# Tap matrices of a depthwise convolution: laid out on the host and loaded by GpSimd's queue, in place of a VectorE product

## What is computed

```
def _causal_depthwise_conv(x, w):
    k = w.shape[0]
    return lax.conv_general_dilated(
        x, w[:, None, :], window_strides=(1,), padding=[(k - 1, 0)],
        dimension_numbers=("NWC", "WIO", "NWC"), feature_group_count=x.shape[-1])
...
def conformer_conv(x, w_in, w_dw, b_dw, ln_g, ln_b, w_out):
    a, gate = jnp.split(x @ w_in, 2, axis=-1)
    u = a * jax.nn.sigmoid(gate)
    u = _causal_depthwise_conv(u, w_dw) + b_dw
    u = jax.nn.silu(_layer_norm_2(u, ln_g, ln_b))
    return u @ w_out
```

## Time and profile before

| | |
|---|---|
| runs, median (lowest to highest) | 1764.91 us (1762.72 to 1766.04) |
| the profiled execution's own time | 1764.59 us |
| its span in the trace | 1762.6 us |
| granted TensorE clock, mean | 0.975 of full speed |
| TensorE (PE) busy | 1657.1 us, 94% |
| VectorE (DVE) busy | 1373.8 us, 78% |
| ScalarE (ACT) busy | 1031.0 us, 58% |
| GpSimd (POOL) busy | 48.3 us, 3% |

### The profile page before, as it was taken

The page is one execution under the profiler, slowest core; times in us unless marked ns, Lnnn a source line. Parts: engine busy times, 40 slices in busy tenths (PEclk is TensorE's granted clock), DMA queues, the critical chain, the costliest instruction groups (busy, mean ns, idle before and its releaser), DMA issues.

```text
span 1762.6 us, 22524 instructions
## 1 busy us (share of the span) xinstructions
PE 1657.1 (94%) x9022; PEld 1378.5 (78%) x9022; DVE 1373.8 (78%) x1252; ACT 1031.0 (58%) x901; POOL 48.3 (3%) x44
## 2 busy tenths in 40 slices
PE   2999999988989999998899999999999999999976
PEld 2988678868869998896788777887778877788754
DVE  7786666675875555668788989989899898988986
ACT  2344344463324333434577887778887788877862
POOL 0000002000000000000100000000000000000010
PEclk8999999999999999999899999999999999999998
DMA  9688245704745646453799999999999999999992
GB/s 365 224 338 332 96 155 190 288 1 159 205 177 209 251 157 237 180 215 144 267 404 370 408 414 418 406 388 416 415 415 409 399 408 405 417 408 378 411 413 98
DMA packets 119663, 528.30 MB, mean 300 GB/s; under 512 B 10288, under 2 KB 16704, under 8 KB 76288
## 3 DMA queue, kind: packets, MB, share of 16 engines
q1 hardware_dynamic: 112704, 512.44, 74.9%
q10 hardware_dynamic: 5520, 9.62, 1.5%
q0 software_dynamic: 1328, 4.73, 0.7%
HBM read 519.84 MB, written 14.25 MB: 303 GB/s over the span
## 4 chain that ended last, share of the span: by engine, by line
PE 59%; DVE 11%; DMA 5%; ACT 3%; issue 1%; POOL 0%; SPq 0%; DVEq 0%; POOLq 0%; ACTq 0%
PE psum L932 15%; PE psum L934 15%; PE psum L933 15%; DVE units L2029 7%; DMA ring<-in_experts 5%; PE psum L1348 3%; PE psum L1349 2%; ACT units L1838 2%; PE psum L1411 1%; PE psum L1259 1%; PE psum L1463 1%; PE psum L1370 1%; PE psum L1400 1%; DVE R L2429 0%; PE psum L1212 0%
## 5 line engine op out<-in xcount | busy, mean ns | idle before, releaser
L2029 DVE TENSOR_TENSOR units<-ring,units 128x2048 fp32r<-128x2048 f32 (+1 forms) x439 | 990.1, 2280 | 232.2 <-ACT units L1566 134.8
L1838 ACT CAST units<-ring 128x2048 fp32r<-128x2048 f32 x320 | 609.5, 1914 | 184.7 <-PE psum L934 108.3
L1566 ACT CAST units<-ring 128x2048 fp32r<-128x2048 f32 (+1 forms) x119 | 218.5, 1880 | 215.3 <-PE psum L934 185.7
L932 PE MATMUL psum<-units,xr 128*128 128x512 f32 x672 | 268.1, 399 | 7.6 <-DVE units L2029 6.1
L934 PE MATMUL psum<-units,xr 128*128 128x512 f32 x672 | 263.6, 392 | 0.0
L933 PE MATMUL psum<-units,xr 128*128 128x512 f32 x672 | 263.6, 392 | 0.0
L932 PE MATMUL psum<-xr,units 128*128 128x256 f32 x864 | 249.1, 288 | 4.5 <-DVE xr L2029 3.2
L933 PE MATMUL psum<-xr,units 128*128 128x256 f32 x864 | 248.0, 287 | 0.0
L934 PE MATMUL psum<-xr,units 128*128 128x256 f32 x864 | 247.9, 287 | 0.0
L932 PE MATMUL psum<-units,H 128*128 128x512 f32 x472 | 186.5, 395 | 4.4 <-DVE H L2029 4.4
L934 PE MATMUL psum<-units,H 128*128 128x512 f32 x472 | 185.0, 392 | 0.0
(11 more groups left out here) (326 smaller groups left out, 1661.4 us busy)
## 6 DMA issues: line engine op xcount, KB each, us to landing
ring<-in_experts SPq DMA_DIRECT2D x336, 1024.0 KB, 10.8
ring<-in_mod_w SPq DMA_DIRECT2D x12, 2048.0 KB, 10.0
ring<-in_ret_w_in SPq DMA_DIRECT2D x11, 2048.0 KB, 10.0
ring<-in_fox_w_in SPq DMA_DIRECT2D x8, 2048.0 KB, 8.7
ring<-in_sc_w_in SPq DMA_DIRECT2D x6, 2048.0 KB, 8.1
ring<-in_ffn_w_gate SPq DMA_DIRECT2D x5, 2048.0 KB, 7.8
ring<-in_ffn_w_up SPq DMA_DIRECT2D x5, 2048.0 KB, 7.9
ring<-in_ffn_w_down SPq DMA_DIRECT2D x5, 2048.0 KB, 9.1
```

What stands on the lines that cost most here:

```text
L932: mm(dst, left[0], right[0], start=first, stop=False)
L1566: nc.scalar.copy(dst[0], src).then_inc(unit_high, 3 - len(parts))
L1838: nc.scalar.copy(dst, src).then_inc(unit_high, 1)
L2029: return v.tensor_tensor(dst, src, high.bitcast(F32), ALU.subtract)
```

## The change

The host now lays out the diagonal matrices of all 8 blocks, zeros included, as 8 arrays of 128 by 1024 numbers without the factor 0.5. GpSimd's queue loads those of blocks 2 to 7 into `diags`, each 512 KB, with one semaphore for each of the two buffers. n = 0 and 1 are loaded once bank `conf_g` 0 is filled, n = 2 to 5 once the bank of block n - 2 is filled. VectorE's six products, ScalarE's load of 144 KB and the wait for it are gone. ScalarE applies the factor 0.5 as the `scale` of the activation that it does anyway.

```
     taps = taps.transpose(1, 4, 2, 3, 0).reshape(P, KB * STACK * GROUPS)
-    half = np.tile(0.5 * np.eye(QUAD, dtype=np.float32), (STACK, 1))
-    return np.ascontiguousarray(np.concatenate([half, taps], axis=1))
+    laid = np.zeros((P, KB, STACK * GROUPS, QUAD), np.float32)
+    p = np.arange(P)
+    laid[p, :, :, p % QUAD] = taps.reshape(P, KB, STACK * GROUPS)
+    return np.ascontiguousarray(laid.transpose(1, 0, 2, 3).reshape(KB, P, STACK * GROUPS * QUAD))
...
-                pe.wait_ge(diag_ready, n + 1)
+                pe.wait_ge(diag_loaded[n % DIAGS], 16 * (n // DIAGS + 1))
...
-            act.dma_start(gate[:, 0:QUAD + KB * STACK * GROUPS], t["conv_taps"]).then_inc(taps_loaded, 16)
...
                 nc.scalar.activation(conv[:, k8, :], bank("conf_taps", k8)[:, 0:T], ACT.Identity,
-                                     bias=vec[:, k8, V_CB:V_CB + 1]).then_inc(emptied["A"], 1)
+                                     scale=0.5, bias=vec[:, k8, V_CB:V_CB + 1]).then_inc(emptied["A"], 1)
...
+                if name == "final_1":
+                    pool.wait_ge(bank_filled, BANK_AT["conf_g", 0] + 1)
+                    for n, k8 in enumerate(CONV_BY_TENSOR):
+                        if n >= DIAGS:
+                            pool.wait_ge(bank_filled, BANK_AT["conf_taps", k8 - DIAGS] + 1)
+                        pool.dma_start(diags[:, n % DIAGS].rearrange("p n c -> p (n c)"), t["conv_taps"][k8]
+                                       ).then_inc(diag_loaded[n % DIAGS], 16)
...
-            def diagonals(n):
-
-                k8 = CONV_BY_TENSOR[n]
-                if n >= DIAGS:
-                    dve.wait_ge(bank_filled, BANK_AT["conf_taps", k8 - DIAGS] + 1)
-                shape = [P, STACK * GROUPS, QUAD]
-                v.tensor_tensor(diags[:, n % DIAGS], quad_ident.unsqueeze(1).to_broadcast(shape),
-                                quad_taps[:, k8].unsqueeze(2).to_broadcast(shape), ALU.mult
-                                ).then_inc(diag_ready, 1)
...
-                    dve.wait_ge(taps_loaded, 16)
-                    for n in range(DIAGS):
-                        diagonals(n)
...
-                n = DIAGS + (k - early) // 4
-                if (k - early) % 4 == 3 and n < len(CONV_BY_TENSOR):
-                    diagonals(n)
```

More of the change, by code:

```diff
@@ L522, in build @@
         stacked = region(8448, len(CONV_BY_TENSOR), STACK, SPAN)
-        quad_ident = gate[:, 0:QUAD]
-        quad_taps = gate[:, QUAD:QUAD + KB * STACK * GROUPS].rearrange("p (k n) -> p k n", k=KB)
         row_g, row_b = region(11264, D), region(14336, D)
@@ L621, in build @@
         conv_ready = sem("conv_ready")
-        diag_ready = sem("diag_ready")
+        diag_loaded = [sem(f"diag_loaded{i}") for i in range(DIAGS)]
         stacked_in = {g: sem(f"stacked{g}") for g in range(CONV_BY_VECTOR // 2, KB // 2)}
         rows_out = {g: sem(f"rows_out{g}") for g in range(CONV_BY_VECTOR // 2, KB // 2)}
-        taps_loaded = sem("taps_loaded")
         lg_ready = sem("lg_ready")
```

## The result

The changed kernel takes 1771.37 us (median of 6 runs, 1770.09 to 1773.37) against 1764.24 us before: ratio 1.0033, 95% interval 1.0022 to 1.0045. It is slower by 0.2 to 0.45%, and lies inside the stated range (1764.0 to 1772.5), 3.2 us above the likeliest value. A second comparison gave 1771.73 against 1765.3 us, ratio 1.0042 (1.0027 to 1.0057).

What follows compares the result with a forecast made beforehand. TensorE's tap matmuls were taken as the bound, not VectorE; late loads of blocks 3 and 5 add 3.4 us to 1764.59, giving 1768.0, or 1768.2 us as a median. Range 1764.0 to 1772.5 us.

Steps and rivals of the forecast that it cites:

- What bounds the stretch: Convolution: TensorE's six blocks bound it, not VectorE; removing two products ahead of the taps (2.27 us) gains 0.06 us.
- The mechanism: Blocks 2 to 5: each load waits for block n - 2, due 3.45 us later; waits 0.5 to 6 us over before, chance 0.70.
- The rival of loads in time: Blocks 2 to 5 do not wait for loads; gain at most 0.82 + 0.06 us, time 1764.0 to 1765.8; chance 0.15.
- L(2): Time for block 2's load to land, issued at 474.08 near quiet: 4.3 us, start 478.4.
- L(3): Time for block 3's load to land, issued at 477.53 into full DMA engines: 5.75 us, start 483.3.
- L(4): Time for block 4's load to land, issued at 482.1 beside the 2 MB ring load: 6.6 us, start 488.7.
- L(5): Time for block 5's load to land, issued at 487.0 as the ring load ends: 5.75 us, start 492.75.
- its formula: Tap matmuls: change in time is L(3) + L(5) - 8.1 us, while blocks 3 and 5 wait for their own loads.
- The clock: Rival: TensorE's clock falls to 1.2 GHz in the new gaps, +3.5 to +7 us; with long loads, chance 0.12.
- Loads pushing back the shifted loads: Before block 4: two new loads at 1.3 us each delay SP's shifted loads by 2.6 us, to 487.7; not deciding.
- Downstream: Behind the convolution: transposes, statistics, root and normalization run in sequence, so the 3.4 us delay passes on whole.
- The forecast's own list of signs: In the trace: landings 4 to 7 us, gaps before blocks 2 to 5, transposes 2 to 5 us later; wrong if clock falls.

Runs made afterwards that it cites:

- e6_hybrid: Changed kernel with only blocks 0 and 1 loaded, VectorE still making blocks 2 to 5; ratio to before 0.9998, tanh of `conf_g` 0 to first transpose 62.7 us.
- e9_quiet: Changed kernel with four blocks loaded to separate places ahead of SP's shifted loads, blocks 4 and 5 made by VectorE; ratio to before 0.9997, stretch 62.0 us.
- e1_six: Changed kernel with a place of its own for nearly every block, each load issued 14 us or more before its matmuls; ratio to before 1.0023, stretch 66.3 us.
- e3_ringlate: Changed kernel with SP's 2 MB ring load issued only after the last tap block is multiplied; ratio to before 1.0028, stretch 69.9 us.
- e5_idle: Kernel before plus four 512 KB loads on GpSimd's queue to a place nothing reads, VectorE still making the diagonals; ratio to before 1.0028, stretch 68.5 us.
- e7_gap: Kernel before with block 4 made to wait for block 5's product, no traffic added; ratio to before 1.0026, stretch 68.8 us.
- e2_actq: Changed kernel with its six loads issued by ScalarE's queue instead of GpSimd's; ratio to before 1.0032, stretch 72.1 us.

## Why the prediction was right, and where its sizes were off

*What bounds the stretch* held. VectorE's place on the chain from 448 to 470 us was not worth 2.3 us: the first tap matmul still waits 0.86 us and begins 41.14 us after the tanh before and after, so not even the 0.06 us can be seen. SP's store moved up by 0.74 us (465.36 before, 463.64 + 0.98 = 464.62 after) where the working had 0.8. What the working missed is that VectorE's later products are worth nothing only under the cover of the gap before block 4: e6_hybrid closes that gap, and 0.54 us of waiting for the last product comes up. So the ceiling of 0.88 us on the gain was too low; e9_quiet is 1.7 us below before in the stretch.

*The mechanism* held: a load issued only when block n - 2 is done is late, three of four times; e1_six issues the loads early, and no gap is ended by a load any more. A fourth gap, before block 5, was forecast and did not come: its load landed at 487.55 + 7.1 = 494.65, while block 4 still ran. The rival of loads in time is refuted by the 4.04 us gap.

*The number* was right by the width of the range. By medians the change costs 7.1 us where the forecast had 3.3; it lies in the range because that reached 4.3 us above the likeliest value. What came was the waits at nearly their upper end (5.9 us over before, of 0.5 to 6) together with a fallen clock, and the forecast gave each a chance of its own but not the two at once.

*The terms that were mis-sized.* L(2) = 4.3 and L(3) = 5.75 measured 4.5 and 6.6; L(4) = 6.6 measured 9.1 and L(5) = 5.75 measured 7.1 us. The fourth was the one that counted: the forecast let the odd blocks make the longer chain and put block 4 at 488.7, which is 487.7 in the time of this execution; it began at 491.27. The row of 6.6 us that it was sized by was the first of two loads of 512 KB that ScalarE issued together at 735 us beside the ring's loads; the second of them took 8.0 us in the same trace, a row that the working left out and that lay closer. In the changed kernel shifted loads, two loads of taps and a ring load stood in the engines together. e3_ringlate shows the ring load's part, 3.8 of the 9.1 us. The form of the sum was sound: with the measured landings its formula gives 6.6 + 7.1 - 8.1 = 5.6 us, and the chain over blocks 2 and 4 gives 5.5, close to the 5.9 us of gaps. A smaller term was off in every round trip: GpSimd issued its load 3.98 us after the start of a block, and not after the 3.73 us that ScalarE's rows gave, and the block started 0.1 to 0.2 us behind the landing. The row of 3.7 us, read as a load with little beside it, has a DMA share of 0.71 around it; the sum did not use it.

*The clock* was written as a rival, with the gaps adding up to 5 us and a price of 3.5 us or more. It was a part of what happened, at 1.7 us in one execution and 2.5 in the other, and it does not take several gaps: in e5_idle and e7_gap it comes with a single one. The longest gap in the forecast's own sum was the 1.95 us before block 4 (488.7 - 486.75), and by the rows below no fall goes with that; so the missing clock term comes out of the mis-sized L(4). Over the tap matmuls of the twelve traces, no gap up to 2.25 us was followed by a fall, and those of 2.65, 2.76, 3.06, 3.29, 3.31, 3.42, 3.79, 3.98 and 4.04 us were; one of 3.38 us (e2_actq, before block 3) was not, and what made it different stays open.

*Loads pushing back the shifted loads* was in the working as 2.6 us for block 4, where it did not decide since block 4's own load was later (the last shifted load had landed by 485.8 at the latest). e1_six and e5_idle show it at 1.2 and 2.0 us of gap where it does decide. To take the wait for the loads away and leave their traffic where it is does not mend the change: e1_six is still 2.6 us over before.

*Downstream* the working passed the delay on whole. It did not arrive whole: the root "conf" stands 7.07 us later than before (503.92 against 496.85), the next root, of the layer behind, only 6.17 us later (530.47 against 524.30). In the 8 us behind "conf" the clock was different, here before and after:

```profile
499.00:507.00 8.00, 6.39 (x25) 5.27 (x26) 5.26 (x10) 5.47 (x10) 0.00 (x0) 0.60 0.01 2
```

```profile
506.00:514.00 8.00, 6.17 (x28) 5.53 (x29) 4.17 (x9) 5.58 (x10) 0.00 (x0) 0.79 0.01 2
```

In this execution the clock was back at 1.00 before the first matmul of `conf_w_out` (511.28); before, it was 0.50 over the first nine of them, until 507. That gave back 0.9 us. It is not shown to belong to the change: the work between the two roots is the same in all twelve traces, and it took 26.5 us in both executions of the changed kernel, 27.4 us before and 28.5 us in e6_hybrid.

*The forecast's own list of signs.* Held: six loads, gaps before blocks 2, 3 and 4, the earlier emptying and store, the taps done by 486. Missed: landings reached 9.1 us where 4 to 7 were given; there was no gap before block 5; the transposes came 7.1 us later (500.01 against 492.94) where 2 to 5 were given; and one of the signs of being wrong appeared, a clock below 1 before 495 (0.50 from 492.5).

## What to carry to other kernels

A buffer pair that was deep enough for a producer of 1.2 us is not deep enough for a load: compare the landing time under the traffic of that very moment, not the quiet one, with the work of one buffer, and issue the load so early that its landing does not matter: in e9_quiet 8.6 us of landing cost nothing with 20 us of lead. A load that nobody waits for still delays the load beside it that somebody waits for. And a gap in TensorE's work has two prices, its own length and the lower clock behind it.

## What the runs showed of the hardware that was not expected

- Of the late loads of 512 KB, the first took 4.1 to 4.5 us with little beside it, the second 5.6 to 7.9 us beside the shifted loads, the third 9.1 to 10.2 us beside shifted loads and a 2 MB ring load, and the fourth 6.8 to 7.7 us beside the rest of that ring load (the changed kernel twice, e5_idle, e2_actq; the same on GpSimd's queue and on ScalarE's). Without the ring load the third and fourth took 5.3 and 4.0 us (e3_ringlate). Even the first two loads of the changed kernel, at 429 us beside each other and one ring load, took 7.6 and 9.4 us. The Trainium skill, "DMA: Bandwidth & Descriptors", section on the anatomy of a DMA on the gpsimd path, would have 3.2 us (2.0 us plus bytes over 436 GB/s, an estimate for 512 KB). These runs do not agree: 4.0 to 4.5 us with little beside it on that queue, and 5.6 to 9.3 us, up to nearly three times the figure, beside other transfers.
- A gap of 2.5 us more in TensorE's work, with no transfer added (e7_gap), cost 5.1 us, with a granted clock of 0.56 to 0.58 in the windows from 484 to 492 us.
- A single profiled execution can hide what the median shows, and the other way: e7_gap's profile has a span of 1763.5 us, only 0.9 us over before's, with a median 5.0 us higher, and a stretch 5.1 us longer. What lies before the stretch varied by over 5 us between executions (the tanh at 427.0 to 432.1 us).
